# Retention and the last output projection: from two stages to one, ordered by head

## The reference, cut to what matters

```python
def step(S, inp):                       # one chunk of 128 tokens, per head
    qc, kc, vc = inp
    o_inter = jnp.einsum('bhtk,bhkv->bhtv', qc, S) * q_decay
    scores = jnp.einsum('bhtk,bhsk->bhts', qc, kc) * intra_decay[None]
    o_intra = jnp.einsum('bhts,bhsv->bhtv', scores, vc)
    S_new = chunk_decay * S + jnp.einsum('bhsk,bhsv->bhkv', kc * k_decay, vc)
    return S_new, o_inter + o_intra
...
o = rms_norm(o).reshape(b, t, W_C) * jax.nn.silu(g.astype(f32))
return o.astype(h.dtype) @ w_out, s_new    # w_out: 2048 x 1024; then y = y + this
```

## Time and profile before

| | us |
|---|---|
| median of 3 runs (lowest, highest) | 2333.31 (2330.46, 2337.14) |
| the profiled execution's own time | 2327.28 |
| its span, first to last instruction | 2325.2 |
| PE busy in the span | 1992.4 (86%) |
| DVE, POOL, ACT busy | 897.6, 659.7, 531.7 |
| mean granted TensorE clock | 0.915 |
| HBM read and written | 186.91 MB, 88.08 MB: 118 GB/s |

### The profile page before, as it was taken

One profiled execution on the slowest core, in us unless ns is written; L12 is line 12 of the kernel. 1 busy time (PEld: TensorE's weight loads), 2 busy tenths in 40 slices (PEclk: granted clock), 3 DMA queues, 4 the chain that ended last, 5 costly groups with the idle time before them and its releaser, 6 DMA issues. The chain is left out here.

```text
span 2325.2 us, 28346 instructions
## 1 busy us (share of the span) xinstructions
PE 1992.4 (86%) x10186; PEld 1578.0 (68%) x10186; DVE 897.6 (39%) x1336; ACT 531.7 (23%) x989; POOL 659.7 (28%) x550
## 2 busy tenths in 40 slices
PE   5999999778887837886948999999999588986999
PEld 4789998644444526764838999887888455555786
DVE  5640000277874449762246443111000156554110
ACT  3210100256654332322121000000111244332000
POOL 2422230056551026522022332222330122216000
PEclk9999999898889967877979999999999789997999
DMA  4332231323323650114443243222321689866320
GB/s 134 111 98 80 77 105 47 113 84 90 117 90 97 199 178 2 58 59 145 149 140 95 75 117 106 80 83 80 98 84 43 205 277 303 291 223 245 109 81 27
DMA packets 205240, 278.75 MB, mean 120 GB/s; under 512 B 27284, under 2 KB 145492, under 8 KB 201812
## 3 DMA queue, kind: packets, MB, share of 16 engines
q1 hardware_dynamic: 130420, 183.79, 25.0%
q10 hardware_dynamic: 72256, 84.70, 11.0%
q0 software_dynamic: 2464, 8.91, 1.1%
HBM read 186.91 MB, written 88.08 MB: 118 GB/s over the span
## 5 line engine op out<-in xcount | busy, mean ns | idle before, releaser
L241 PE MATMUL odd_bank<-odd_w_hi,odd_h_hi 128*128 128x512 f32 (+1 forms) x576 | 224.5, 390 | 1.1 <-DVE odd_stage_tm L453 1.1
L241 PE MATMUL odd_bank<-odd_w_lo,odd_h_hi 128*128 128x512 f32 (+1 forms) x576 | 224.4, 389 | 0.0
L241 PE MATMUL odd_bank<-odd_w_hi,odd_h_lo 128*128 128x512 f32 (+1 forms) x576 | 224.1, 389 | 0.0
L1699 PE MATMUL out_bank<-out_w_hi,out_m_hi 128*128 128x512 f32 (+1 forms) x432 | 136.8, 399 | 54.0 <-DVE out_w_lo L1769 47.6
L222 POOL CAST odd_w_hi<-odd_raw 128x1024 fp32r<-128x1024 f32 x48 | 53.3, 1110 | 399.3 <-PE odd_bank L241 333.7
L1699 PE MATMUL out_bank<-out_w_hi,out_m_lo 128*128 128x512 f32 (+1 forms) x432 | 135.6, 395 | 0.0
L1699 PE MATMUL out_bank<-out_w_lo,out_m_hi 128*128 128x512 f32 (+1 forms) x432 | 135.4, 395 | 0.0
L1699 PEld LDWEIGHTS out_bank<-out_w_hi,out_m_hi 128*128 128x128 f32 (+1 forms) x432 | 80.2, 187 | 75.2 <-issue 48.1
L241 PE MATMUL odd_bank<-odd_h_hi,odd_w_hi 128*128 128x362 f32 (+1 forms) x384 | 127.9, 333 | 1.5 <-DVE odd_h_lo L424 1.5
L241 PE MATMUL even_bank<-even_h_hi,even_w_hi 128*128 128x362 f32 (+1 forms) x384 | 126.2, 329 | 1.6 <-DVE even_stage_tm L453 1.6
L241 PE MATMUL odd_bank<-odd_h_hi,odd_w_lo 128*128 128x362 f32 (+1 forms) x384 | 127.3, 332 | 0.0
(11 more groups left out here) (274 smaller groups left out, 4068.5 us busy)
## 6 DMA issues: line engine op xcount, KB each, us to landing
odd_raw<-in_w_in_odd SPq DMA_DIRECT2D x48, 512.0 KB, 4.0
even_raw<-in_w_in_even SPq DMA_DIRECT2D x32, 512.0 KB, 4.0
k_page<-in_cache_k SPq DMA_DIRECT2D x64, 256.0 KB, 3.1
v_page<-in_cache_v SPq DMA_DIRECT2D x64, 256.0 KB, 3.0
rt_s<-in_state_ret SPq DMA_DIRECT2D x32, 512.0 KB, 6.0
out_ret_sample<-rt_s ACTq DMA_DIRECT2D x32, 512.0 KB, 4.8
v_tm<-odd_stage_tm ACTq DMA_DIRECT2D x64, 128.0 KB, 1.9
g_tm<-odd_stage_tm ACTq DMA_DIRECT2D x64, 128.0 KB, 1.9
```

Source lines behind the costliest of these rows:

```text
L241: mm = pe.matmul(out, stationary, moving, start=(j == 0), stop=(j == len(pairs) - 1))
L1699: mm = pe.matmul(bank[slot][n][0:r, :], m, w[:, c, n * 512:n * 512 + 512], start=(c == 0 and j == 0), stop=(c == K - 1 and j == 2))
```

## The change

Retention and the projection "out1" become one stage, `retention_out`; `retention` only keeps its arguments until `project_out` is called. The 32 steps now run head by head (`h, c = divmod(n, NCH)`), with one state in SBUF. After its other work, step n multiplies the mix of step n-2 with the 512 rows of the weights that belong to its head (`product_out`: 24 products of 512 columns in two halves, one PSUM bank each), and DVE adds the two halves to y, which stays in SBUF for all 9 token tiles and holds the residual from the start; SP stores it in the last head. The mix is no longer written to DRAM: ACT rounds the turned output from `tr`, DVE takes the rest (`round_mix`, `split_mix`). The weights of one head at a time are in SBUF, split in its step 1 by ACT, DVE and POOL.

The samples' outputs now come per head and group of four sequences: 8 units, made in steps 2, 6, 10 and so on in the bank that the next step does not use, and turned in the step after, behind that step's own `turn_out`. `turn_out` waits for `m_split` of the unit before instead of for the copy. The tile `square` is gone: the norm's squares go to the slot of `og` that the gate then fills, so that the norm waits until that slot's unit of two before has been turned. All seven `stack` calls come in steps 0 to 3, two in a step. The stores of the sample states move from ACT's queue to SP's. q and k are laid out by head (`by_head`), and loads are per step: 128 KB each of q and k, 256 KB of v and g, in three slots. The loads of y's tiles 3 to 8 come after step 3, since these tiles first hold the samples' split keys and values. ACT's rounding of the keys in `prepare` waits for DVE's scores, since the two now share a bank.

```diff
--- before.py
+++ after.py
-def by_chunk(x):
+def by_head(x):
...
+    nr = x.shape[0] // (HC * P)
+    prompt = full[0:x.shape[0] * TP].rearrange("(h p c r t) -> h p c r t", p=P, h=HC, r=nr, t=P)
+    sample = full[x.shape[0] * TP:].rearrange("(p h r t) -> h p r t", p=P, h=HC, r=nr)
     return prompt, sample
...
+    if tag == "out1":
+        retention_out(nc, *_held.pop("retention"), weight, x_of, y_of)
+    else:
+        project_out_alone(nc, tag, mix_fm, weight, x_of, y_of)
...
+def retention_out(nc, q_fm, k_fm, v_tm, g_tm, state_in, state_prompt, state_samples, mix_fm, consts, weight, x_of, y_of):
...
+        yp = [ps("y0", [P, 512]), ps("y1", [P, 512])]
...
+        state = sb("state", [P, J, DV])
...
+        m_hi, m_lo = sb("m_hi", [P, 2, R, P], F32R), sb("m_lo", [P, 2, R, P], F32R)
+        ms_hi, ms_lo = sb("ms_hi", [P, R, TS], F32R), sb("ms_lo", [P, R, TS], F32R)
+        raw = sb("raw", [P, R, D])
+        w_hi, w_lo = sb("w_hi", [P, R, D], F32R), sb("w_lo", [P, R, D], F32R)
+        y = sb("y", [P, NT, D])
...
+            units.append(("step", n))
+            if n % SEQS == 2:
+                units.append(("samples", n // SEQS))
+        unit_of = {x: m for m, x in enumerate(units)}
+        outs = [(n // NCH, t) for n in range(NSTEP) for t in ((6, NT - 1) if n % NCH == 6 else (n % NCH,))]
+        out_of = {x: i for i, x in enumerate(outs)}
...
+            more = [unit_of["samples", (n - 1) // SEQS]] if (n - 1) % SEQS == 2 else []
+            return [unit_of["step", n - 1]] + more
+        def outs_in(n):
+            return [] if n < 2 else [x for x in outs if x[0] == (n - 2) // NCH and x[1] == (n - 2) % NCH or
+                                     (n - 2) % NCH == 6 and x == ((n - 2) // NCH, NT - 1)]
...
             load_qk(0)
+            load_v(0)
...
+            load_g(0)
+            for n in range(SEQS):
+                load_s0(n)
+            load_raw(0)
+            load_qk(2)
+            load_v(2)
             load_g(1)
+            load_g(2)
+            for t in range(3):
+                load_y(t)
             for grp in range(NGRP):
...
+            for n in range(NSTEP):
+                h, c = divmod(n, NCH)
+                if n + NQ < NSTEP:
+                    sp.wait_ge(kt_done, n + 1)
+                    sp.wait_ge(qd_done, qd_until(n))
+                    load_qk(n + NQ)
+                if n + NV < NSTEP:
+                    sp.wait_ge(v_split, n + 1)
+                    load_v(n + NV)
+                    sp.wait_ge(gated, unit_of["step", n] + 1)
+                    load_g(n + NV)
+                sp.wait_ge(s1_done, J * (n + 1))
+                sp.dma_start(state_samples[c, h].rearrange("(j k) v -> k j v", k=P), s1[n % 2][:]).then_inc(s1_left[n % 2], 16)
...
+                if n == SEQS - 1:
+                    for seq in range(NS):
+                        sp.wait_ge(stacked[seq], NSTACK)
+                    for t in range(3, NT):
+                        load_y(t)
...
+                    sp.dma_start(state_prompt[h].rearrange("(j k) v -> k j v", k=P), state[:]).then_inc(state_left, 16)
+            for h, t in outs[-NT:]:
+                sp.wait_ge(added, 2 * out_of[h, t] + 2)
+                sp.dma_start(y_of(t), y[0:rows_of(t), t, :]).then_inc(y_left, 16)
...
+                for r in range(1, R, 2):
+                    pool.wait_ge(w_rounded, R * h + r + 1)
+                    nc.gpsimd.tensor_tensor(w_lo[:, r, :], raw[:, r, :], w_hi[:, r, :].bitcast(F32), ALU.subtract).then_inc(w_split_p, 1)
...
+                if n == 1:
+                    split_weights(0)
+                if n >= NCH and (n - 2) % NCH == 1 and n > NCH + 2:
+                    split_weights((n - 3) // NCH)
...
                 pe.wait_ge(gated, m + 1)
                 if m:
-                    pe.wait_ge(tr_read, m)
...
+                for r in range(R):
+                    part = og[:, m % 2, r * P:r * P + P]
+                    if units[m][0] == "step":
+                        mm = pe.transpose(tr[:, r, :], part, ident[:])
+                    else:
...
+            def sample_outputs(h, grp):
+                m = unit_of["samples", h * NGRP + grp]
+                pe.wait_ge(gated, m - 1)
+                for s in range(SEQS):
+                    pe.wait_ge(s0_in[s], 16 * (h * NGRP + grp + 1))
+                rows, out = slice(grp * ROWS, (grp + 1) * ROWS), o[m % 2]
+                for s in range(SEQS):
+                    pe.matmul(out[s * ROWS:(s + 1) * ROWS, :], scm_s[rows, h, rows], v_s[rows, h], start=True, stop=False,
+                              skip_group_check=True, tile_position=(grp * ROWS, s * ROWS))
                 for j in range(J):
...
+                    for s in range(SEQS):
+                        mm = pe.matmul(out[s * ROWS:(s + 1) * ROWS, :], qd_s[:, h, j, rows], s0[s][:, j], start=False,
+                                       stop=(j == J - 1), skip_group_check=True, tile_position=(0, s * ROWS))
+                mm.then_inc(o_done, 1)
...
+            def product_out(h, t):
+                n_out, rows = out_of[h, t], rows_of(t)
+                m = unit_of["step", h * NCH + t] if t < NCH else unit_of["samples", h * NGRP + 1]
+                pe.wait_ge(m_split, m + 1)
+                hi, lo = (m_hi[:, t % 2], m_lo[:, t % 2]) if t < NCH else (ms_hi[:], ms_lo[:])
+                for half in range(2):
+                    cols = slice(half * 512, half * 512 + 512)
+                    if n_out:
+                        pe.wait_ge(added, 2 * (n_out - 1) + half + 1)
+                    for r in range(R):
+                        if half == 0 and t == 0:
+                            pe.wait_ge(w_split_p if r % 2 else w_split_d, R // 2 * h + r // 2 + 1)
+                        for j, (a, b) in enumerate(((hi, w_hi), (hi, w_lo), (lo, w_hi))):
+                            mm = pe.matmul(yp[half][0:rows, :], a[:, r, :], b[:, r, cols], start=(r == 0 and j == 0),
+                                           stop=(r == R - 1 and j == 2))
+                        if half == 1 and t == NCH - 1 and r < R - 1:
+                            mm.then_inc(w_used, 1)
+                    mm.then_inc(full, 1)
...
+                for x in turned_in(n):
+                    if units[x][0] == "samples":
+                        pe.wait_ge(picked, SEQS)
+                    turn_out(x)
...
+                if n < NCH:
+                    pe.wait_ge(stacked[n], NSTACK)
...
+                for x in outs_in(n):
+                    product_out(*x)
+            for n in range(NSTEP, NSTEP + 2):
+                for x in turned_in(n) if n == NSTEP else ():
+                    turn_out(x)
+                for x in outs_in(n):
+                    product_out(*x)
...
+                nc.scalar.copy(v_hi[:, n % 2], v[:, n % NV]).then_inc(v_rounded, 1)
-                act.wait_ge(kt_done, n + 1)
-                nc.scalar.activation(kd_hi[:, n % 2], kt[:], ACT.Copy, scale=k_dec[:, h:h + 1]).then_inc(kd_rounded, 1)
                 act.wait_ge(scm_done, n + 1)
+                nc.scalar.activation(kd_hi[:, n % 2], kt, ACT.Copy, scale=k_dec[:, h:h + 1]).then_inc(kd_rounded, 1)
                 nc.scalar.copy(scm_hi[:, n % 2], scm[:, n % 2]).then_inc(scm_rounded, 1)
...
+            def norm(m):
                 at = slice(m % 2, m % 2 + 1)
-                if m:
-                    act.wait_ge(sq_done, m)
+                act.wait_ge(o_done, m + 1)
                 if m >= 2:
-                    act.wait_ge(gated, m - 1)
-                nc.scalar.activation(square[:], src, ACT.Square, accum_out=ss[:, at]).then_inc(sq_done, 1)
+                    act.wait_ge(tr_done, m - 1)
+                nc.scalar.activation(og[:, m % 2, :], o[m % 2][:], ACT.Square, accum_out=ss[:, at]).then_inc(sq_done, 1)
...
+            def round_mix(m):
+                kind, n = units[m]
+                if kind == "step" and n >= 2:
+                    act.wait_ge(full, 2 * out_of[(n - 2) // NCH, (n - 2) % NCH] + 2)
+                elif kind == "samples" and n >= NGRP:
+                    act.wait_ge(full, 2 * out_of[n // NGRP - 1, NT - 1] + 2)
+                hi, _, src = parts_of(m)
                 act.wait_ge(tr_done, m + 1)
+                nc.scalar.copy(hi, src).then_inc(m_rounded, 1)
+            def round_weights(h):
+                for r in range(R):
+                    if h and r < R - 1:
+                        act.wait_ge(w_used, (R - 1) * (h - 1) + r + 1)
+                    elif h:
+                        act.wait_ge(full, 2 * out_of[h - 1, NCH - 1] + 2)
+                    act.wait_ge(raw_in[r], 16 * (h + 1))
+                    nc.scalar.copy(w_hi[:, r, :], raw[:, r, :]).then_inc(w_rounded, 1)
...
+            round_weights(0)
             for n in range(NSTEP):
+                norm(unit_of["step", n])
+                for seq in range(2 * n + 1, min(2 * n + 3, NS)):
+                    stack(seq)
                 if n + 2 < NSTEP:
                     prepare(n + 2)
```

(46 more changed lines are left out.)

364 lines of the change are left out of this document (149 added, 215 removed).

## The result

The changed kernel takes 2356.59 us (median of 4 runs, 2354.89 to 2358.39), the kernel before 2333.74 (4 runs): ratio 1.0098, 95% interval 1.008 to 1.0115. It is slower by 22.9 us; 11.3 were forecast.

A forecast was written before the change was run, and what follows sets the result against it. PE's work and its losses (64.8 us) were taken as the bound. Late start, steps, products, waits and clock summed to 453.5 us from 1883.7, against 441.5: 12 more, 2339, plus 6.0 for the median: 2345 us, range 2315 to 2366.

The forecast's parts named there:

- The wait: Before the second turn, once in four steps: PE idles 4.4 us uncovered, bounds 2.1 and 5.5; seven make 30.8 us.
- either link: Serial chain between two turns: second turn waits for `m_split`; norm waits for the first turn to free its `og` slot.
- The clock after it: After each 4.4 us wait of PE: 2.5 us lost to a lower clock, ends 0 and 3; seven make 17.5.
- clock up: Rival, chance 0.17: the clock stays up after the waits between products, 20 us go, 2325.
- The second turn: Samples' units turned on PE's path, 8 instead of 2: 0.4 us each; turns 3.3 us in the sum.
- The start: Before step 4: it begins at 1916.3 instead of 1883.7, 32.6 us later, ends 20 and 45.
- after the preparation that ended at 1851.4: Before the loop: ACT rounds four weight tiles, 4.2 us, after that preparation, and hardly waits for their loads.
- two each, 8.5 us: Steps 0, 1 and 2: two `stack` calls each keep ACT 8.5 us, ahead of the rounding DVE needs.
- The head's change: At three head changes DVE waits for the store of the state: up to 1 us, 3 in all.
- The cover: End of every step: 5.41 us of products let DVE finish early, removing most of 18.3 us of retention waits.
- Transfers: Rival, chance 0.05: small loads make transfers the bound, 118 us more, 2463.
- A wait in every step: Rival, chance 0.15: DVE's longer queue makes PE wait 0.7 us in each step, 20 us more, 2365.

The follow-up runs named there:

- mix first: Changed kernel with squares in their own tile and, in steps with two turns, the first unit's mix rounded and split ahead of `prepare`: 2323.6 us, ratio 0.9955.
- tables first: Changed kernel with the samples' small table loaded first and the four tables in one DMA instead of four: 2357.7 us, ratio 1.011.
- small loads: Changed kernel with each load of q, k, v and g issued as two of half the partitions: 2358.4 us, ratio 1.0111.
- a third of the products: Changed kernel with only the rounded-by-rounded part of each output product, 8 products instead of 24: 2267.4 us, one run.

## Why the prediction was right and wrong

Direction and mechanism were right. The size was not: 12 us more were forecast from step 4 of before on, and the tail has 27.5. Of the 15.5 between them 11.6 are one term, the start. The terms:

**The wait, right.** "4.4 us": 4.46, released by DVE's split, ACT's square released by PE's turn; taking away either link shortened it as its price said.

**The clock after it, mis-sized.** "I take 2.5": 3.48 in each of six steps, about 1.7 in step 31 (13 us at 0.87), 5.1 us more in all. The "1.0 per wait" that the rival "clock up" was measured against was the mean of two kinds of wait in before, of nothing and of some 1.6 us, and rows 2 count ten such waits, not eight; in the run with the mix first 1.64 us cost 2.34.

**The second turn, mis-sized.** "I take 0.4": a step with a second turn and no wait takes 12.03 against 11.23, so 0.8, 2.8 us more in seven.

**The start, mis-sized.** "32.6 us later" was 44.2. The step that failed first is "after the preparation that ended at 1851.4": I carried over the start of before and priced the new loading of the tables (two DMAs with the small table first became six with it last) at nothing. That preparation ends 34.9 us after the last product of the stage ahead, where it was 29.4; step 0 starts 6.2 us later, and tables first gives 5.8 of them back (small loads 4.7, with the tables' order unchanged). Next, "two each, 8.5 us": twelve issues took 9.6 and 11.1 us, and `u` of step 2 came 8.3 us later than worked out, 2.1 on top of the 6.2. The other 3.3 us came in step 3: 1.34 of wait for keys, 0.4 more in the wait before the second turn (8.64 us, 8.2 by my times, with a stack call in it), and 10.2 instead of 9.0 from there to step 4. That the start was held by three things in a row, ACT's issues, the tables and behind them SP's order of keys, I did not see: taking the first two away moved the wait to the third.

**The head's change**, "up to 1 us, 3 in all": 0.13 each in the changed kernel (14.99 us a step, 14.86 by my rows), since the wait of 4.46 lies ahead of it; 18.6 with that wait gone. It was priced by landing alone, and SP's program order was left out. That is -2.6 in the sum.

From step 4 on the forecast was 453.5 - 32.6 = 420.9, measured 424.8: 3.9 more, namely clock 5.1, turns 2.8, heads -2.6, waits 29.7 instead of 30.8, the end 5.0 us after the last product instead of 6.1, and 0.8 over the other steps. That these nearly cancel is luck. So 12 + 11.6 + 3.9 = 27.5, the tail's measured difference. By medians it is 22.9 against 11.3; the profiled execution of before lay 6 us under its median, so the tails may overstate the difference.

**The cover**: the waits for the sample state are gone, also with a third of the products. That it is the products that remove them was not shown, since no run was without any. **Transfers**: refuted from step 4 on, by the small loads. **A wait in every step**: refuted, ordinary steps take 11.22 us where 5.75 + 5.41 = 11.16 were forecast.

## What to carry to other kernels

When a stage is rebuilt, work its first microseconds anew from the new issue order, and follow each queue in program order past every wait in it: a transfer's time to land (4.2 us here) says little if it is issued 9.2 us late. When one wait is removed, list what it was covering; here two kinds, the state's store and the keys, came up one after the other, 18.6 and 12 to 22 us. And a wait of TensorE of a few microseconds is to be priced with the clock that may follow it, 2.3 to 3.5 us each on the mean of these steps, so that a serial chain belongs beside products even if it is short.

## What the runs showed of the hardware that was not expected

The lost clock after a wait of 1.6 to 4.5 us does not follow from its length: on the mean 2.34, 2.62 and 3.48 us after 1.64, 3.15 and 4.46, but 0.26 to 3.4 after the same 1.64, and in the kernel before some 1.6 after 2.06 and nothing after 2.53. Leaving out two thirds of the output products lowered the clock from step 4 on from 0.94 to 0.87, so that part of the saving was given back. Halving the loads to 64 and 128 KB changed no ordinary step. An issue of a stack call on ACT's queue took 0.63 us at best and up to 2.3 in the start, at a DMA share of 0.79. With the same six issues of tables PE's first product of the stage came 13.2 us after the stage's first DMA issue where SP's loads of the states were issued meanwhile, and 8.8 us after it where they were issued later.
